# Layer norms in pairs of feature tiles: one VectorE instruction for two neighbouring tiles, with mean and 1/std read through a broadcast

## What is computed

```python
h = layer_norm(concat([meta, x]), ln_in_g, ln_in_b)
h = layer_norm(DN_ALPHA * h + 0.5 * swiglu(h, ffn1_w_gate, ffn1_w_up, ffn1_w_down), ffn1_ln_g, ffn1_ln_b)
h = layer_norm(DN_ALPHA * h + token_mixer(h, w_in, ..., w_out), mix_ln_g, mix_ln_b)
h = layer_norm(DN_ALPHA * h + 0.5 * swiglu(h, ffn2_w_gate, ffn2_w_up, ffn2_w_down), ffn2_ln_g, ffn2_ln_b)
return h[:, N_META:]
```

## Time and profile before

| | us |
|---|---|
| median of 3 runs | 1182.48 (1182.23 to 1184.0) |
| the profiled execution, its own time | 1184.65 |
| its span, from the first to the last instruction | 1182.9 |
| PE busy | 1087.4 (92%) |
| DVE busy | 744.3 (63%), 1254 instructions |
| ACT busy | 413.8 (35%) |

### The profile page before, as it was taken

The page is one execution under the profiler, slowest core; times in us unless marked ns, Lnnn a source line. Parts: engine busy times, 40 slices in busy tenths (PEclk is TensorE's granted clock), DMA queues, the critical chain, the costliest instruction groups (busy, mean ns, idle before and its releaser), DMA issues.

```text
span 1182.9 us, 20793 instructions
## 1 busy us (share of the span) xinstructions
PE 1087.4 (92%) x8724; PEld 895.5 (76%) x8724; DVE 744.3 (63%) x1254; ACT 413.8 (35%) x571; POOL 34.4 (3%) x95
## 2 busy tenths in 40 slices
PE   3799999999899979999998988969999999989995
PEld 2488888888688837898775555847888888868884
DVE  7666656668666576646454556676565656876645
ACT  3722222235211177634215442164222222541115
POOL 1000000000000000000000000000000000000000
PEclk9899999999899989999656998989999999999998
DMA  4222322223222202313000001112322222222202
GB/s 145 70 107 106 106 75 103 106 103 115 98 99 89 71 1 72 107 37 108 1 1 1 1 1 37 72 36 72 107 106 85 92 106 106 98 98 99 98 1 71
DMA packets 26472, 88.98 MB, mean 75 GB/s; under 512 B 3003, under 2 KB 7443, under 8 KB 26419
## 3 DMA queue, kind: packets, MB, share of 16 engines
q1 hardware_dynamic: 25408, 87.24, 21.1%
q10 hardware_dynamic: 1011, 1.00, 0.3%
HBM read 86.13 MB, written 2.10 MB: 75 GB/s over the span
## 4 chain that ended last, share of the span: by engine, by line
PE 41%; DVE 6%; ACT 5%; issue 1%; ACTq 0%; POOL 0%; DVEq 0%
PE PS L463 16%; PE PS L497 13%; PE PS L736 2%; PE PS L655 2%; PE PS L753 2%; ACT H L833 1%; DVE wsp L1158 1%; PE PS L651 1%; DVE cmax L1136 1%; PE PS L452 1%; PE PS L751 1%; ACT wsp L839 1%; PE PS L718 1%; PE PS L695 1%; ACT xs L831 1%
## 5 line engine op out<-in xcount | busy, mean ns | idle before, releaser
L463 PE MATMUL PS<-xs,wsp 128*128 128x264 f16 x4224 | 485.6, 279 | 16.4 <-ACT xs L831 10.5
L463 PEld LDWEIGHTS PS<-xs,wsp 128*128 128x128 f16 x4224 | 415.3, 99 | 87.0 <-issue 6.9
L839 ACT ACTIVATE wsp<-stage,wscale 128x2048 f16<-128x2048 f32 (+2 forms) x73 | 156.5, 2144 | 358.0 <-DVE wscale L1122 182.8
L1158 DVE SCALAR_TENSOR_TENSOR wsp<-stage,wscale,wsp 128x2048 f16<-128x2048 f32 (+2 forms) x73 | 184.6, 2529 | 128.3 <-ACT wsp L839 128.3
L497 PE MATMUL PS<-big,wsp 128*128 128x264 f16 x2112 | 242.4, 278 | 11.0 <-DVE big L1234 9.5
L497 PEld LDWEIGHTS PS<-big,wsp 128*128 128x128 f16 x2112 | 207.5, 99 | 45.8 <-DVE big L1234 10.3
L1136 DVE TENSOR_REDUCE cmax<-stage 128x1 f32<-128x2048 f32 (+2 forms) x73 | 179.7, 2461 | 3.9
L1170 DVE SCALAR_TENSOR_TENSOR big<-PS,oscale,tmp_a 128x528 f32 (+1 forms) x44 | 33.7, 766 | 83.0 <-ACT tmp_a L846 83.0
L846 ACT ACTIVATE tmp_a<-PS,oscale 128x528 f32<-128x528 f32 x44 | 30.8, 700 | 142.7 <-PE PS L463 142.7
L555 PE MATMUL PS<-xs,wsp 128*128 128x264 f16 x576 | 65.8, 276 | 0.4 <-ACT big L901 0.4
L555 PEld LDWEIGHTS PS<-xs,wsp 128*128 128x128 f16 x576 | 56.0, 98 | 10.0 <-issue 1.7
(11 more groups left out here) (176 smaller groups left out, 825.9 us busy)
## 6 DMA issues: line engine op xcount, KB each, us to landing
stage<-in_gate SPq DMA_DIRECT2D x44, 512.0 KB, 3.8
stage<-in_up SPq DMA_DIRECT2D x44, 512.0 KB, 4.6
stage<-in_down SPq DMA_DIRECT2D x32, 704.0 KB, 4.9
stage<-in_w_in SPq DMA_DIRECT2D x16, 512.0 KB, 4.7
stage<-in_w_out SPq DMA_DIRECT2D x8, 512.0 KB, 4.6
X<-in_xT SPq DMA_DIRECT2D x2, 1056.0 KB, 7.1
stage<-in_w_in SPq DMA_DIRECT2D x2, 576.0 KB, 4.3
out_T<-H SPq DMA_DIRECT2D x8, 132.0 KB, 1.8
```

Of the source, the lines that this page charges most:

```text
L463: return nc.tensor.matmul(PS[:, 4 * s + 2 * g + h, 0:HALF], w, xs[:, xp, k, token_half(h)], start=k == 0 and wp + xp == 0, stop=k == KD - ...
L839: nc.scalar.activation(wsp[:, slot, 0, 0:cols], stage[:, slot, 0:cols], ACT.Copy, scale=wscale[:, slot:slot + 1]).then_inc(w_hi, 1)
L1158: nc.vector.scalar_tensor_tensor(wsp[:, slot, 1, 0:cols], stage[:, slot, 0:cols], wscale[:, one], wsp[:, slot, 0, 0:cols], ALU.mult, ALU.s ...
```

## The change

Three places handle the tiles k and k + 1 by one instruction of twice the width (528 elements for each partition, in two runs of 264): the subtraction of the mean, the multiplication by 1/std, and the low part. The mean (in PSUM) and 1/std (in SBUF) have 264 elements and are read twice through a broadcast. Each instruction raises its semaphore by 2 when it has ended, and the low part waits for both tiles of `H`. ACT's and PE's programs are unchanged: they still go tile by tile and wait for each tile's count.

```diff
             def centre(L, h):
                 dve.wait_ge(mean_ready, 2 * L + h + 1)
-                for k in range(KD):
-                    x = X[:, k, token_half(h)]
-                    nc.vector.tensor_tensor(x, x, PS[:, h, 0:HALF], ALU.subtract).then_inc(centred, 1)
+                mean = PS[:, h, 0:HALF].unsqueeze(1).to_broadcast([P, 2, HALF])
+                for k in range(0, KD, 2):
+                    x = X[:, k:k + 2, token_half(h)]
+                    nc.vector.tensor_tensor(x, x, mean, ALU.subtract).then_inc(centred, 2)
...
                 def split_lo(h, k):
-                    dve.wait_ge(h_ready, ln_step(L, h, k) + 1)
-                    nc.vector.scalar_tensor_tensor(xs[:, 1, k, token_half(h)], H[:, k, token_half(h)], xscale[:, L:L + 1],
-                                                   xs[:, 0, k, token_half(h)], ALU.mult, ALU.subtract).then_inc(x_ready, 1)
+                    t = token_half(h)
+                    dve.wait_ge(h_ready, ln_step(L, h, k) + 2)
+                    nc.vector.scalar_tensor_tensor(xs[:, 1, k:k + 2, t], H[:, k:k + 2, t], xscale[:, L:L + 1],
+                                                   xs[:, 0, k:k + 2, t], ALU.mult, ALU.subtract).then_inc(x_ready, 2)
...
                 for h in range(2):
...
-                    for k in range(KD):
-                        x = X[:, k, token_half(h)]
-                        dve.wait_ge(centred, ln_step(L, h, k) + 1)
-                        nc.vector.tensor_tensor(x, x, rstd[:, token_half(h)], ALU.mult).then_inc(normed, 1)
+                    rstd_2 = rstd[:, t].unsqueeze(1).to_broadcast([P, 2, HALF])
+                    for k in range(0, KD, 2):
+                        x = X[:, k:k + 2, t]
+                        dve.wait_ge(centred, ln_step(L, h, k) + 2)
+                        nc.vector.tensor_tensor(x, x, rstd_2, ALU.mult).then_inc(normed, 2)
                         if k >= 2 and L < 3:
                             split_lo(h, k - 2)
                     if L < 3:
                         split_lo(h, KD - 2)
-                        split_lo(h, KD - 1)
```

More of the change, by code:

```diff
@@ L1097, in split_lo @@
                 def split_lo(h, k):
-                    dve.wait_ge(h_ready, ln_step(L, h, k) + 1)
-                    nc.vector.scalar_tensor_tensor(xs[:, 1, k, token_half(h)], H[:, k, token_half(h)], xscale[:, L:L + 1],
-                                                   xs[:, 0, k, token_half(h)], ALU.mult, ALU.subtract).then_inc(x_ready, 1)
+                    t = token_half(h)
+                    dve.wait_ge(h_ready, ln_step(L, h, k) + 2)
+                    nc.vector.scalar_tensor_tensor(xs[:, 1, k:k + 2, t], H[:, k:k + 2, t], xscale[:, L:L + 1],
+                                                   xs[:, 0, k:k + 2, t], ALU.mult, ALU.subtract).then_inc(x_ready, 2)
                 for h in range(2):
+                    t = token_half(h)
                     dve.wait_ge(std_ready, 2 * L + h + 1)
-                    nc.vector.reciprocal(rstd[:, token_half(h)], std[:, token_half(h)]).then_inc(rstd_ready, 1)
+                    nc.vector.reciprocal(rstd[:, t], std[:, t]).then_inc(rstd_ready, 1)
                     dve.wait_ge(rstd_ready, 2 * L + h + 1)
-                    for k in range(KD):
-                        x = X[:, k, token_half(h)]
-                        dve.wait_ge(centred, ln_step(L, h, k) + 1)
-                        nc.vector.tensor_tensor(x, x, rstd[:, token_half(h)], ALU.mult).then_inc(normed, 1)
+                    rstd_2 = rstd[:, t].unsqueeze(1).to_broadcast([P, 2, HALF])
[3 more added lines that the diff above has]
+                        nc.vector.tensor_tensor(x, x, rstd_2, ALU.mult).then_inc(normed, 2)
                         if k >= 2 and L < 3:
```

## The result

| | kernel before | with pairs |
|---|---|---|
| median of the runs shown with the result, us | 1182.36 (1182.23 to 1184.0, 4 runs) | 1192.12 (1185.89 to 1193.14, 4 runs) |
| the profiled execution, us | 1184.65 | 1185.89 |
| its span, us | 1182.9 | 1184.1 |

What follows compares the result with a forecast made beforehand. PE was taken to bound the stages between the layer norms, so its later starts come out at the end. The layer norms' 0.42 + 2.12 + 1.11 + 0.29 = +3.94 on the median 1182.48 gave 1186.4 us, range 1183.2 to 1188.7.

Steps and rivals of the forecast that it cites:

- first layer norm: Faster centre gains 0.40 before ACT's weight chunk; longer low parts and first multiplied pair delay PE's second tile: +0.42 us.
- fourth: Last layer norm, no low parts: only the first square's delay reaches the last store, +0.29 us.
- Second: Layer norm before the projections: ACT's half 1 at +0.84, PE's wait for the first low-part pair 1.28 longer: +2.12 us.
- projection tile not PE-bound: Rival: PE's clock is up sooner, second layer norm costs about 1.1, sum +2.9, 1185.4 us; chance 0.14.
- Third: Layer norm after the mixer: delays 0.29, 0.27, 0.28, 0.27 up to DVE's chunk_lo, which ends last: +1.11 us.
- The cover of 0.17: Third layer norm: PE's idle time before its second tile, 1.18 before the change, shrinks to 0.17 us.
- the 2.0 in that figure: DVE busy time claimed saved by the 64 instructions merged out of 128, part of about 7 us in all.
- the 0.05 a pair: DVE time freed by merging two centre instructions: 2 x 0.34 - 0.63 = 0.05 us.
- one stretch more: Clock rival: one more half-clock stretch for eight tiles between the layer norms, 1.68 us, giving +5.6, 1188.1; chance 0.10.
- faster: Rival: later start lets the clock rise in the mixer's second stretch, -7.2, sum -3.2, 1179.2 us; chance 0.07.
- This stage hardly wanders: Mixer: argument against the clock rising there, since three runs lay within 1.8 us.
- The rejected rule on PSUM sources: Fixed 120 cycles per PSUM instruction, 58 for SBUF: merged centre pair saves 125 ns, whole at +3.3 us.

Runs made afterwards that it cites:

- The kernel with single edges: Kernel before with pairs only in mid-run; tiles 0, 1 single in subtraction and multiplication, 0, 1, 6, 7 in the low part: 1182.50 us, ratio 0.9998.
- the short and the long execution: Two traced executions of the same changed kernel, pairs in all three places of every layer norm: 1185.89 us and 1191.65 us.
- the delay of 2.50: Kernel before, no pairs, plus an unread 390-column reciprocal ahead of half 1's own in the second layer norm: median 1187.13 us, ratio 1.0059.
- a bare delay: Kernel before, no pairs, plus an unread reciprocal of 150 to 510 columns in the second layer norm: medians 1186.18, 1185.08, 1187.13, 1187.61 us.
- pairs and delay: Changed kernel plus about 1.0 us of unread reciprocal in the second layer norm: 1186.89 us (1.0029), on another chip 1187.07 us (1.0037).
- A delay of 1.00: Kernel before, no pairs, plus an unread 150-column reciprocal ahead of half 1's own in the second layer norm: median 1186.18 us, ratio 1.0029.
- one of 1.93: Kernel before, no pairs, plus an unread 300-column reciprocal ahead of half 1's own in the second layer norm: median 1185.08 us, ratio 1.0019.

## Why the prediction was wrong

- **The direction and its mechanism were right.** Nearly all of DVE's saving is off the path, and whoever waits for one tile waits for two. The kernel with single edges agrees with it from the other side.
- **The terms:** first layer norm +0.42 forecast, +0.42 and +0.31 traced; fourth +0.29 against +0.30 and +0.35. That the first agrees to the hundredth is luck: the same stage took 57.53 to 58.75 in six traces without pairs in it. Second +2.12 against +2.32: the turn from half 0 to half 1 was 0.12 longer and the wait for the low part 0.07. Its part that was bound by PE held (8.40 for 8.36), so the rival "projection tile not PE-bound" falls. Third **+1.11 against +1.45 and +2.77**: the turn again, and the sums of squares, which took 5.54 and 6.86 for 5.38 in the kernel before, since PE stood at half clock for longer. This term was mis-sized by ignoring that the sums are at PE's clock, though the earlier trace rows showed both speeds. The cover of 0.17 ahead of PE's second tile was no thinner than forecast: DVE's chunk_lo was still what PE waited for, by 0.96 and 0.42 us. DVE's busy time fell by 9.4 and not by 7; the 2.0 in that figure doesn't follow from the 0.05 a pair (64 pairs would give 3.2). Beyond the 0.40 in the first layer norm none of it counted.
- **The step that failed** is the first: "a microsecond by which PE starts later behind a layer norm comes out at the end". In the projections and the mixer it does not: the same instructions took 312.2 to 318.2 us in the traces, by where the half clock lay, which is more than the whole forecast. The premise came from the earlier trace rows, which leave out 566 to 764, most of that stretch. I had the clock as two rivals, "one stretch more" (0.10, +1.68) and "faster" (0.07), each with one change of clock at one place. Between the short and the long execution there are four: 1.7 in the projections, 2.9 near 640, 1.4 near 703, 1.3 in the third layer norm, less 0.4 at 632 and 0.6 near 723, where the short one's clock is the lower. "One stretch more" gave 1188.1 where 1191.5 was seen.
- **A second assumption failed with it:** "The durations are those of an execution 2.17 above the median; I take the differences as the same". Against the traced execution before, the long one is +7.0: 3.94 as forecast, 1.66 more in the third layer norm, 1.25 in the mixer, and 0.15 in the rest. Against the medians most executions are 8 to 9 us slower. The last 1.4 to 2.3 us are the traced execution's distance from its kernel's medians. No execution nearer to them was traced. But the kernel with pairs in the last two is the kernel before up to the third layer norm, and its traced execution (1183.46) took 313.06 where the traced one before took 316.88, so the distance may well lie in the mixer.
- **"This stage hardly wanders"** was read from three runs within 1.8 us. All 108 runs before bear it out for that kernel's total, and it did not carry over to the changed one.
- **The rule and the rows.** The rejected rule on PSUM sources would have made the first layer norm 0.6 cheaper: it came out at the row's price, four pairs of the first centre taking 18.53 - 16.06 = 2.47 from start to the next instruction, 0.62 each. The rule that idle time halves the clock and sustained work restores it (the Trainium skill, TensorE: Matmul & The Clock Gate, Part 1) fits the sums of squares behind idle time, but not the earlier trace rows: there PE was busy for 29.73 of 30 us and the granted clock stayed at 0.50. The measurement decides, and no run here shows what tips it.

**What stays open.** Why the clock's changes lie at other places against the program from one execution to the next was not found, nor why no execution of the kernel before is a long one. The traces show that the changes lie alike within a group: the first fall in the mixer is 50.3 behind L555 in both long executions with pairs, and 117.7 to 118.0 behind it in the three short ones. No trace was obtained of the three executions at 1197 with the delay of 2.50. And that the pairs make long executions frequent rests on counts, here of runs at 1187.5 or above: 13 of 19 with pairs everywhere, 4 of 8 with pairs in the first two layer norms, 6 of 8 with the low part in pairs, 1 of 12 with 1/std, none of 11 with the mean, 2 of 12 with pairs in all but the second, none of 10 in the last two, none of 11 with single edges; with a bare delay 1 of 6, 2 of 11, 5 of 11 and 4 of 5 (1.00 to 3.25); 4 of 13 with pairs and delay; none of 108 before.

## What to carry to other kernels

Merging two instructions saves only their fixed part (0.06 us for a pair of tensor_tensor here, 0.14 for one of low parts) and delays the first result by a whole tile (0.28), so merge in the middle of a run and leave the first and last instruction single wherever another engine waits for them. Behind such a change look also at the unchanged stages where PE's granted clock is below one: where the clock's changes fall against the stage can cost or give several us there (312 to 318 for the same instructions here), more than the change itself, and it differs between executions of one program. A median of a few runs then says little before one execution of each group of times has been traced.

## What the chip showed that was not expected

- A tensor_tensor that reads one operand twice through a broadcast is no slower than one with two full operands: 703 ns from SBUF and 696 from PSUM for 528 columns, against 708.
- Adding 1.0 us of work to the kernel with pairs removed all executions of 1190 and more (0 of 13, where 13 of 19 were).
- A delay of 1.00 cost 3.2 us, one of 1.93 cost 2.1 (on another chip), both against the kernel before beside them.
- Two executions of the changed kernel whose L555 began at 452.81 and 452.93 took 313.10 and 318.05 us from there to the third mean.
- The same 46 matmuls behind the second layer norm took 7.59 to 9.65 us in the traces of these kernels: 7.59 with the low part in pairs, 8.31 to 8.48 in most, 9.65 with 1/std in pairs.
